# Compression of the cached keys and values: contraction over 128 partitions, and no block of its own

## The reference, cut to what matters

```python
sb = raw.reshape(b, n_sb, CMP_STRIDE, N_KV_HEADS, HEAD_DIM)      # groups of 16 tokens
for r in range(CMP_RATIO):                                        # 2 halves of a block of 32
    pr = jnp.einsum('bnskd,sde->bnke', sb + per[r][None, None, :, None, :], w1r[r])
    parts.append(pr[:, r:r + nc])
h = sum(parts[1:], parts[0])
return jnp.einsum('bnke,ef->bnkf', jax.nn.gelu(h), w2)
```

## Time and profile before

| | |
|---|---|
| median of the runs | 1499.1 us |
| profiled execution, first to last instruction (its span) | 1497.9 us |
| PE busy | 1463.4 us, 98% |
| DVE busy | 865.1 us, 58% |
| ACT busy | 419.7 us, 28% |
| mean granted clock of PE | 0.998 of full |
| compression stage, 169.2 to 262.3 us | PE products 512 records of 64 x 256 and 128 of 64 x 128; 34 turns |

### The profile page before, as it was taken

The page is one execution under the profiler, slowest core; times in us unless marked ns, Lnnn a source line. Parts: engine busy times, 40 slices in busy tenths (PEclk is TensorE's granted clock), DMA queues, the critical chain, the costliest instruction groups (busy, mean ns, idle before and its releaser), DMA issues. The chain is left out here.

```text
span 1497.9 us, 26053 instructions
## 1 busy us (share of the span) xinstructions
PE 1463.4 (98%) x9875; PEld 1225.9 (82%) x9875; DVE 865.1 (58%) x1907; ACT 419.7 (28%) x1063; POOL 363.4 (24%) x479
## 2 busy tenths in 40 slices
PE   8999999999999999999999999999999999999998
PEld 7877899755557888888888889788888888888888
DVE  2754443888554795654767735661585556776513
ACT  3011343788520533324200001442531111000012
POOL 0000300467640369991230034370000000000000
PEclk9999999999999999999999999999999999999999
DMA  8346561311595444463344310712312221322201
GB/s 275 113 126 144 166 217 51 92 59 51 160 351 140 154 169 161 142 229 131 118 133 133 119 66 32 307 46 78 113 57 91 78 105 65 112 85 85 84 28 59
DMA packets 142895, 184.38 MB, mean 123 GB/s; under 512 B 31298, under 2 KB 101642, under 8 KB 141746
## 3 DMA queue, kind: packets, MB, share of 16 engines
q1 hardware_dynamic: 139634, 174.31, 35.5%
q0 software_dynamic: 3136, 8.39, 1.7%
HBM read 163.42 MB, written 29.69 MB: 129 GB/s over the span
## 5 line engine op out<-in xcount | busy, mean ns | idle before, releaser
L2683 POOL TENSOR_SCALAR att_p<-att_p,att_tot,gates 128x128 f32<-128x128 f32 (+3 forms) x128 | 79.1, 631 | 45.2 <-DVE att_tot L2605 44.6
L305 PE MATMUL psum<-xT,l_w 128*128 128x260 f32 x384 | 85.3, 383 | 2.0 <-PEq L113 1.8
L1010 PE MATMUL psum<-xT,l_w 128*128 128x260 f32 x384 | 85.2, 383 | 1.6 <-PEq L113 1.6
L305 PEld LDWEIGHTS psum<-xT,l_w 128*128 128x128 f32 x384 | 72.8, 190 | 13.5 <-issue 2.4
L1010 PEld LDWEIGHTS psum<-xT,l_w 128*128 128x128 f32 x384 | 72.8, 190 | 12.9 <-issue 1.8
L1026 PE MATMUL psum<-l_up_t,l_w_sums 128*128 128x260 f32 x336 | 78.2, 382 | 0.0
L2205 PE MATMUL psum<-cmp_xt,cmp_w 64*128 64x256 f32 (+1 forms) x640 | 72.2, 362 | 0.3 <-DVE cmp_xt L2126 0.3
L1026 PEld LDWEIGHTS psum<-l_up_t,l_w_sums 128*128 128x128 f32 x336 | 63.8, 190 | 9.8
L2656 ACT ACTIVATE att_p<-att_p,att_low 128x128 f32<-128x128 f32 (+3 forms) x128 | 70.5, 554 | 2.8 <-DVE att_low L2596 2.8
L1289 ACT ACTIVATE l_hidden<-l_tmp 128x260 f32<-128x260 f32 x64 | 26.6, 420 | 144.9 <-DVE l_tmp L1439 144.8
L2596 DVE CUSTOM_DVE_ANT_0 att_p<-psum,causal 128x128 f32<-128x128 f32 (+3 forms) x128 | 55.7, 486 | 18.7 <-PE psum L2428 18.3
(11 more groups left out here) (607 smaller groups left out, 3174.5 us busy)
## 6 DMA issues: line engine op xcount, KB each, us to landing
l_w<-in_mlp_w SPq DMA_DIRECT2D x16, 2048.0 KB, 7.9
l_w<-in_mlp_w SPq DMA_DIRECT2D x32, 1024.0 KB, 4.8
proj_w<-in_nsa_w_in SPq DMA_DIRECT2D x4, 2048.0 KB, 10.0
cmp_raw<-in_cache_kv_cmp SPq DMA_DIRECT2D x24, 256.0 KB, 3.2
xT<-in_cache_kv_cmp SPq DMA_DIRECT2D x24, 256.0 KB, 3.0
sa_more<-in_cache_kv_sel POOLq DMA_DIRECT2D x44, 128.0 KB, 5.9
sa_more<-in_cache_kv_sel SPq DMA_DIRECT2D x34, 128.0 KB, 8.4
hT<-in_cache_kv_cmp SPq DMA_DIRECT2D x16, 256.0 KB, 2.9
```

The costliest lines, as they stand in the source:

```text
L305: mm = nc.tensor.matmul(ps[:, n % 8, 0:HALF], w[s][:, k, m * P:(m + 1) * P], src[:, kk, cols(h)], start=(kk == 0), stop=(kk == last))
L1010: mm = nc.tensor.matmul(ps[:, n % 8, 0:HALF], w[s][:, k, m * P:(m + 1) * P], src[:, kk, cols(h)], start=(kk == 0), stop=(kk == last))
L2683: ve.tensor_scalar(pr[:, n % PR, par, at:at + w], pr[:, n % PR, par, at:at + w], tot[:, n % PR, u, par:par + 1], c.gates[:, i, gate:gate + ...
```

## The change

**Contraction over 128 partitions.** `xt` is laid out so that partitions 0 to 63 hold the even tokens of a stride and partitions 64 to 127 the odd ones (all four heads side by side in 512 columns), and `cmp_w1` is loaded to match. A sample step has 8 products of 128 rows x 512 columns in one bank instead of 32 products of 64 rows x 256 columns in two. A prompt step has 8 products of 130 columns (2 for the bias). Shift and add are one instruction each over 504 columns. The four banks 4 to 7 are used in turn by four steps.

**Empty.** Each engine now makes four copies per turn, one for each half of the PSUM partitions (h) and each parity of token (o), of 64 partitions x 256 elements.

**Order.** Steps go samples 0 and 1 first, then the prompt, then the other samples. Tails come inside a step, after its second (or third) turn's products, by a table `FINISH`.

**Block.** `stage_compress` becomes a class whose streams run on at the end of the projection's block. The filler products and the barrier between them go. In the last pass POOL scales token tiles 0 and 1; SP issues quads 4 and 5 ahead of the last stores, and waits for all stores before quad 6.

```diff
@@ stage_project, sync
+                    if i == 2:
+                        sp.wait_ge(kv_filled, 7 * 3)
+                        for g in range(4, RQ):
+                            load_quad(c, sp, g)
...
-                c.kv_written = (written, 16 * nrow)
+                sp.wait_ge(written, 16 * nrow)
+                follow.sync(sp)
@@ stage_project, tensor
-                keep_awake(c, 7, 10)
+                pe.wait_ge(gates_kept, QT + 1)
+                pe.wait_ge(row_kept, 3)
+                follow.tensor(pe, kv_joined, kv_scaled, last_scaled)
@@ stage_project, scalar
-                    for at, t in enumerate((2, 3, 0, 1)):
+                    for at, t in enumerate((2, 3, 0, 1) if i < 2 else (2, 3)):
@@ stage_project, gpsimd
+                pool.wait_ge(kv_joined, 7 * 3)
+                for t in range(2):
+                    nc.gpsimd.tensor_scalar(c.kv[:, t, 0, :], c.kv[:, t, 0, :], rs_tok[:, 0, t:t + 1], None, ALU.mult).then_inc(last_scaled, 1)
...
+                follow.gpsimd(pool)
@@ Compress
+    UNITS = (1, 0, 2, 3, 4)
+    FINISH = {4: (0,), 5: (1, 2), 6: (3, 4), 7: (5,), 8: (6,), 9: (7,), 10: (8,)}
@@ empty
-            for hp in range(2):
-                at = hp * nq * w + q * w
-                ins = copy(xt[:, i % 2, :, at:at + w].rearrange("p t (j o x) -> p o t j x", j=4, o=2)[:, z],
-                           ps[:, pair_of(("turn", n)) + z, hp * 2 * P:(hp + 1) * 2 * P].rearrange("p (j x t) -> p t j x", j=4, t=STRIDE))
+        psum = self.c.psum[:, self.pair_of(("turn", n)) + z, :].rearrange("p (x s o) -> p o s x", s=TS, o=2)
+        for h in range(2):
+            for o in range(2):
+                cols = self.xt[o * HD:(o + 1) * HD, i % 2, :, 0:NKV * nq * w].rearrange("p s (a h q j y x) -> p s a h q j y x", a=2, h=2, q=nq, j=4, y=2)
+                ins = copy(cols[:, :, :, h, q, :, z], psum[h * HD:(h + 1) * HD, o])
@@ product
-                    for z in range(2):
-                        moving = xt[z * HD:(z + 1) * HD, i % 2, t, 0:cols]
...
-                        mm = nc.tensor.matmul(out, w1[z * HD:(z + 1) * HD, i % 2, t].rearrange("p r e -> p (r e)"),
-                                              moving, start=(t == 0), stop=(t == STRIDE - 1))
+            mm = nc.tensor.matmul(ps[:, self.sum_bank(i), 0:cols], w1[:, i % 2, t].rearrange("p r e -> p (r e)"),
+                                  xt[:, i % 2, t, 0:cols], start=(t == 0), stop=(t == TS - 1))
@@ tensor, order of PE
+        for i in range(self.STEPS + 1):
+            done, here, tails = 0, range(first[i], first[i + 1]), self.FINISH.get(i, ())
+            for k, n in enumerate(here):
+                turn(n)
+                if i >= 1:
+                    upto = TS * (k + 1) // len(here)
+                    for t in range(done, upto):
+                        product(i - 1, t)
+                    done = upto
+                if 1 <= k <= len(tails):
+                    tail(tails[k - 1])
+            if i == self.STEPS:
+                for t in range(TS):
+                    product(i - 1, t)
+                    if t == TS // 2:
+                        tail(tails[0])
+        keep_awake(c, 4, 8)
+        tail(self.STEPS - 1)
+        keep_awake(c, 4, 4)
@@ scalar
+            for k, n in enumerate(range(self.first[i], self.first[i + 1])):
+                self.empty(act, nc.scalar.copy, n, 1)
+                if 1 <= k <= len(fin):
+                    gelu(fin[k - 1])
+                if k < len(fin):
+                    shift(fin[k])
@@ vector
+                self.empty(dve, nc.vector.tensor_copy, n, 0)
+                if i in (2, 3) and k == 0:
+                    keep_pe(i - 2)
+                if i in (4, 5) and k == 0:
+                    keep_bias(i - 4)
+                if k < len(fin):
+                    add(fin[k])
+                if 2 <= k <= len(fin) + 1:
+                    copy_out(fin[k - 2])
```

More of the change, by code:

```diff
@@ L1583, in _, with stage_project @@
                                         ALU.mult, ALU.add).then_inc(rows_done, 1)
-def stage_project(c):
+def stage_project(c, follow):
     nc, ps = c.nc, c.psum
@@ L1607, in stage_project @@
     gates_filled, gates_kept = c.sem("proj_gates_filled"), c.sem("proj_gates_kept")
-    q_kept, roped = (c.sem(f"proj_{x}") for x in ("q_kept", "q_roped"))
+    q_kept, roped, last_scaled = (c.sem(f"proj_{x}") for x in ("q_kept", "q_roped", "last_rows_scaled"))
     swap_landed = [c.sem(f"proj_swap_landed{s}") for s in range(2)]
@@ L1718, in _ @@
                         load_quad(c, sp, 3)
+                    if i == 2:
+                        sp.wait_ge(kv_filled, 7 * 3)
+                        for g in range(4, RQ):
+                            load_quad(c, sp, g)
                     for n, t in enumerate(TILES_KV):
-                        sp.wait_ge(roped, 8 + i * (QT + 1) + n + 1)
+                        if i < 2:
+                            sp.wait_ge(roped, 8 + i * (QT + 1) + n + 1)
+                        elif t == QT:
+                            sp.wait_ge(row_kept, 3)
+                        elif t >= 2:
+                            sp.wait_ge(kv_scaled, 4 * i + t - 1)
+                        else:
+                            sp.wait_ge(last_scaled, t + 1)
                         if t < QT:
@@ L1889, in _ @@
                             .then_inc(gates_kept, 1)
-                    for at, t in enumerate((2, 3, 0, 1)):
+                    for at, t in enumerate((2, 3, 0, 1) if i < 2 else (2, 3)):
                         act.wait_ge(kv_joined, 7 * i + 6 + at // 2)
                         nc.scalar.mul(c.kv[:, t, b, :], c.kv[:, t, b, :], rs_tok[:, 0, t:t + 1]).then_inc(kv_scaled, 1)
+                follow.scalar(act)
             @block.vector
@@ L1994, in _ @@
                     join_kv(i, b)
-                    for at, t in enumerate(TILES_KV):
+                    for at, t in enumerate(TILES_KV) if i < 2 else ():
                         n = rows_of(t)
@@ L2048, in compress_first_loads @@
     for kv in range(2):
-        w = c.dram["nsa_cmp_w1"][0, kv].rearrange("(r t d) e -> r d t e", r=2, d=HD)
+        w = c.dram["nsa_cmp_w1"][0, kv].rearrange("(r t o d) e -> r o d t e", r=2, o=2, d=HD)
         for r in range(2):
-            for copy in range(2):
-                sp.dma_start(c.cmp_w1[copy * HD:(copy + 1) * HD, kv, :, r], w[r]).then_inc(c.cmp_w_ready, 16)
+            for o in range(2):
+                sp.dma_start(c.cmp_w1[o * HD:(o + 1) * HD, kv, :, r], w[r, o]).then_inc(c.cmp_w_ready, 16)
         for d in range(2):
@@ L3167, in stage_nsa @@
             compress_buffers(c, compress_ctx)
-            stage_project(c)
-            stage_compress(c, cache)
+            follow = Compress(c, cache)
+            stage_project(c, follow)
             compress_ctx.close()
```

417 lines of the change are left out of this document (203 added, 214 removed).

## The result

The changed kernel takes 1528.7 us (median of 4 runs, 1526.5 to 1533.7) against 1501.5 us for the kernel before on the same chip: 1.0187 times as long, 95% interval 1.0170 to 1.0204. The forecast was 1509.1 with a range of 1500 to 1515. The direction was right; the size was not, by 19.6 us.

The account below looks back on a forecast made before the run. PE, busy 98% of the span, was taken as the bound. Seam -2.9, products -4.1 and +0.5, idle time +15.1, clock +1.4 gave +10.0; with span 1497.9 and 1.2 for the median, 1509.1 us, range 1500 to 1515.

Parts of the forecast that it names:

- Seam, -2.9: Between projection and compression: without filler and barrier PE goes on at once, -2.9 us; POOL's scalings 0.85 each.
- Products, -4.1 and +0.5: PE's products: two prompt steps save 4.1 us; eight sample steps save nothing and cost 0.5 more.
- I take 1.45: DVE's four copies emptying a turn: 1.45 us, between bounds of 0.76 and 1.7.
- The slot of 2.28: Steady step on PE: turns start 2.28 us apart, 0.50 of transposes and 1.78 of products.
- It just fits: DVE in a steady slot: copies done 2.18 us after the turn's start, against a slot of 2.28.
- Idle time of PE, +15.1: PE's waits at fill, first tail, later tails and end: 18.8 us, less 3.7 before, so +15.1.
- Clock, +1.4: Half speed over 3.4 us from the idle time before the first tail: +1.4 us, between 0 and 3.
- rival 4: Clock falls more often, at the fill (+1.7) and in thin slots behind turn 13 (+1.7): 1513 us; chance 0.12.
- Rival 1: Copies still hide: stalls at later turns vanish (about -5) and the clock holds (-1.4), 1503 us; chance 0.15.
- rivals 2 and 3: Empties: half the partitions, half the copy, 1497 us, chance 0.08; products: full rows halve product time, 1489 us, chance 0.03.
- Rival 5: SP's load of quad 6, held until all stores land, comes late; 10 us late gives 1514 us; chance 0.05.
- marks set: Profile signs: DVE copies about 415 ns, DVE busy +23 us, records every 430 to 438 ns, steps 10.9 us, clock below 1.

Follow-up runs that it names:

- e_four_full: Changed kernel, but each engine's four copies per turn cover 128 partitions x 256 elements, two into xt, two into a spare buffer: 1520.7 us, ratio 1.0125.
- e_row_halves: Changed kernel, but each 128-row, 512-column product of the last four steps becomes four of 64 rows x 256 columns in two banks: 1526.6 us, ratio 1.0164.
- e_two_rows: Changed kernel with two 128x256 copies per engine and turn, and 64-row x 256-column products in the last four steps: 1507.5 us, ratio 1.0045.
- e_awake: Changed kernel with 128x128 filler matmuls of the identity, into banks nothing reads, where PE waits: 1524.5 us, ratio 1.0156.
- e_old_layout2: Changed kernel with the contraction alone undone, merged block and new order kept, bias as two more columns of the first two steps' products: 1506.2 us, ratio 1.0024.
- e_old_layout: Changed kernel with the contraction undone, merged block and new order kept, bias from 64 small two-column products at the fill: 1516.0 us, ratio 1.0111.

## Why the prediction was wrong, step by step

The forecast had the stage 12.9 us longer (-4.1, +0.5, +15.1, +1.4); it is 30.3 us longer. The steps that failed are three sizes: the set of copies, the slot and the clock. The mechanism (copies lose their cover, PE waits, the clock falls) was right as far as it went; the dearer changeover in each slot was missing from it.

- **Seam, -2.9: right.** The stage starts at 166.28 against 169.23. POOL's two scalings take 1.56 us each, not the 0.85 of the earlier trace rows; in the merged block nothing waits for them.
- **Products, -4.1 and +0.5: right.** Records of 512 columns come every 0.43 us. A product in one matmul over 128 rows is worth no more than two halves side by side.
- **"I take 1.45" for four copies: wrong, 1.73, and the step that cost most.** The row used was of copies that overlap. My upper bound, 1.7 by 418 ns each, was the right one: the sum of four separate durations. ACT's four were put at 1.2 and take 1.50. `e_four_full` has sets of almost the forecast length (1.41), and its stage is 9.1 us shorter than the changed kernel's: over half of the 17.4 us that the forecast missed.
- **The slot of 2.28: wrong, 2.55.** I had counted the products' own time only and taken the changeover from the earlier trace rows, where both kinds of record are 64 rows high. With 128-row products each slot takes 0.27 more, up to 8 us in PE's busy time, and not one of it shows as idle time. It is not 8 us of loss: in place twelve such slots gave back 1.1 us (`e_row_halves`), and 2.7 with shorter copies (`e_two_rows`). Why the change of height costs time, no run here shows.
- **"It just fits" (2.18 against a slot of 2.28): wrong at both ends.** The set ends 2.55 behind the turn's start, but the slot is 2.55 too, so the steady slots hide it all the same.
- **Idle time of PE, +15.1: right in sum, by luck.** It is +16.1 (17.8 less 1.8). The terms: first tail 4.3, found 4.52; turn 13 2.2, found 1.78; first product at 173.1, found 174.46; later turns 0.95, found 1.03. The idle time before was put at 3.7 and is 1.8. But two errors cancel in it, longer copies and a longer slot: with copies near the forecast length (`e_four_full`) the stage has 11.5 us idle, +9.7 and not +15.1.
- **Clock, +1.4: too small.** The clock fell three times, in the fill, about the first tail and at 237; rival 4 had the first, and in part the second. `e_awake` takes 4.5 us off the stage with the clock kept up.

For the fill I had set the start of the trace before against the lower level. That was a misreading. PE's records of that stretch are these, the first of transposes alone:

```profile
5.80 3.67 PE L1758 MATMUL psum<-ident,x_rows 128*128 128x128 f32 x16 [1.85 <-DMA x_rows<-in_x_prompt]
...
9.79 2.47 PE L1758 MATMUL psum<-ident,x_rows 128*128 128x128 f32 x20 [0.31 <-issue]
```

The first sixteen start some 0.22 us apart and last 421 ns each; the 128x128 fillers of the earlier trace rows start 0.11 apart and last 275. That is half the rate, the pace of the 1.2 GHz level, whatever the 1.00 in the clock column says. So no row spoke for a full clock in the fill. That transposes don't count as activity, as the Trainium skill states ("TensorE: Matmul & The Clock Gate", Part 4), is in line with the 0.52 from 171.9 to 178.6, but the gaps between them would do as an explanation too: no run separates the two, and with shorter gaps (0.4 and 0.2 us, `e_old_layout2`) the fill kept 1.00.

By kinds of time the miss looks like this. Busy time: predicted -2.2 (the products and the clock), found +14.2. Of the 16.4 between, the slots explain up to 8. The clock explains about 6: 9.9, less 2.1 for the 4.1 us idle in the first two stretches, less the 1.4 counted. Some 2 are left open. With the idle time's 1.0 that is the trace's 17.4; the rest of the 19.6 is how the medians lie to the profiled spans. This is bookkeeping. What undoing a step gives back are the 9.1, 1.1 and 4.5 us of the runs above, which overlap and don't add.

Rival 1 (copies hide) and rivals 2 and 3 did not occur. Rival 5 did not either: no wait for a page load appears. Rival 4 did, with a price (+3.4 in all) that was too small. Of the marks set, copies at 415 ns, records every 430 ns, 4 us ahead of the first tail and the clock came as said; DVE's +23 us (found +32) and the step's 10.9 us (found 12.6; 9.9, four times 0.27, 1.03 and 0.34 come to 12.35) did not.

## What to carry to other kernels

Before trading two half-height matmuls for one of full height, read the spacing of the halves: at 108 ns against 219 they already share the array, and the trade only moves cost to whoever must now fill both halves. Price a set of copies by whether each starts where the last one did: if they alternate partition halves, take the sum of single durations, not the row of a group that overlaps. Check what stands beside a changed matmul in PE's stream: here a change of height between neighbours cost time that no wait showed, so compare slots, not only idle times. Before you call such a difference a loss, see whether a wait behind it takes it back. And read a clock column together with the spacing of like records.

## What the runs showed of the hardware that was not expected

- ACT's halves take their full length too: four of 64x256 take 1.50 us (367 ns each), where two of 128x256 take 0.65 and four 1.20.
- The changeovers between 64-row transposes and 128-row products take 0.13 and 0.14 us more than those between records of 64 rows, in each of the steady slots.
- Matmuls of 64 rows by 2 columns, all in one half, start 0.11 us apart at the full clock (37 from 167.7 to 171.7 in `e_old_layout`) and 0.21 at the lower level: as slow as those of 64x256 in both halves, 108 ns.
- A wait of 0.92 us behind 47 records of 64 columns was followed by 13 us at the lower level (`e_old_layout2`), and with fillers in its place by none.
- At the start of the trace before, the clock column reads 1.00 while 128x128 transposes run at the pace of the 1.2 GHz level (0.22 us apart).
